# Squares of v summed by transfers, the mixing of gMLP spread over three u chunks, and gelu times mixed v on VectorE

## What is computed

```
z = gelu(rms_norm(x) @ w_in + b_in);  u, v = z[:, :2048], z[:, 2048:]
v = rms_norm(v) * v_gain                     # over the 2048 columns; also an output, for the samples
s[chunk, i, group, d] = sum_j tril(w_s[group])[i, j] * v[chunk, j, group, d] + b_s[group, i]
x = x + (u * s) @ w_out                      # chunks of 128 tokens, 8 groups of 256 columns
```

## Time and profile before

| | us |
|---|---|
| median of 3 runs | 2080.99 |
| the runs | 2080.99, 2080.2, 2087.7 |
| profiled execution, its time | 2089.98 |
| its span, first to last instruction | 2088.1 |
| busy: TensorE, VectorE | 2042.7, 1677.0 |
| busy: ScalarE, GpSimd | 1170.7, 372.2 |

### The profile page before, as it was taken

The page is one execution under the profiler, slowest core; times in us unless marked ns, Lnnn a source line. Parts: engine busy times, 40 slices in busy tenths (PEclk is TensorE's granted clock), DMA queues, the critical chain, the costliest instruction groups (busy, mean ns, idle before and its releaser), DMA issues.

```text
span 2088.1 us, 44481 instructions
## 1 busy us (share of the span) xinstructions
PE 2042.7 (98%) x16512; PEld 1972.9 (94%) x16512; DVE 1677.0 (80%) x2836; ACT 1170.7 (56%) x2101; POOL 372.2 (18%) x413
## 2 busy tenths in 40 slices
PE   9999999989999999999999999999999999999998
PEld 8999999988999999999999999998768889999998
DVE  6779887887477998998899998679665468989997
ACT  5446565666264655655665655445564346656555
POOL 0011111333131111110111111111122121111111
PEclk9999999999999999999999999999999999999999
DMA  5467775664445777775777777451322126777775
GB/s 160 123 162 179 181 184 149 148 152 122 112 112 128 175 179 176 181 186 151 168 177 181 178 186 181 129 138 28 96 72 81 61 61 158 179 184 176 187 181 128
DMA packets 385039, 307.52 MB, mean 147 GB/s; under 512 B 22951, under 2 KB 346836, under 8 KB 384628
## 3 DMA queue, kind: packets, MB, share of 16 engines
q1 hardware_dynamic: 343418, 231.03, 37.0%
q0 software_dynamic: 41152, 74.09, 21.9%
q10 hardware_dynamic: 314, 0.37, 0.1%
HBM read 228.76 MB, written 2.66 MB: 111 GB/s over the span
## 4 chain that ended last, share of the span: by engine, by line
PE 79%; DVE 6%; DMA 6%; issue 4%; ACT 2%; POOL 1%; SPq 1%; DVEq 0%; ACTq 0%; POOLq 0%
PE side L842 29%; PE main L842 20%; PE main L792 16%; DMA raw<-raw 2%; PE side L1389 2%; DVE w_lo L2197 2%; PE main L1151 2%; DMA sums_w<-raw 1%; DMA raw<-in_ffn_w_down 1%; PE main L1319 1%; PE side L1359 1%; POOL tmp_act L3222 1%; DMA raw<-in_ffn_w_gate 1%; PE side L1241 1%; PE main L1221 1%
## 5 line engine op out<-in xcount | busy, mean ns | idle before, releaser
L842 PE MATMUL side<-xw_hi,w_hi 128*128 128x260 f32 x1600 | 455.0, 284 | 20.1 <-DVE v L2347 9.2
L842 PE MATMUL side<-xw_hi,w_lo 128*128 128x260 f32 x1600 | 453.5, 283 | 0.0
L842 PE MATMUL side<-xw_lo,w_hi 128*128 128x260 f32 x1600 | 452.4, 283 | 0.0
L2197 DVE TENSOR_TENSOR w_lo<-raw,w_hi 128x512 fp32r<-128x512 f32 (+2 forms) x540 | 382.8, 709 | 71.0 <-ACT w_hi L1518 22.2
L842 PE MATMUL main<-xw_hi,w_hi 128*128 128x260 f32 x1200 | 341.5, 285 | 0.0
L842 PE MATMUL main<-xw_lo,w_hi 128*128 128x260 f32 x1200 | 338.9, 282 | 0.0
L842 PE MATMUL main<-xw_hi,w_lo 128*128 128x260 f32 x1200 | 338.7, 282 | 0.0
L842 PEld LDWEIGHTS side<-xw_hi,w_hi 128*128 128x128 f32 x1600 | 301.4, 188 | 25.6 <-DVE w_lo L2197 8.5
L842 PEld LDWEIGHTS side<-xw_hi,w_lo 128*128 128x128 f32 x1600 | 301.3, 188 | 0.0
L842 PEld LDWEIGHTS side<-xw_lo,w_hi 128*128 128x128 f32 x1600 | 301.0, 188 | 0.0
L2197 DVE TENSOR_TENSOR w_lo<-sums_w,w_hi 128x1024 fp32r<-128x1024 f32 (+2 forms) x264 | 250.3, 948 | 3.2 <-ACT w_hi L1501 3.2
(11 more groups left out here) (485 smaller groups left out, 4895.2 us busy)
## 6 DMA issues: line engine op xcount, KB each, us to landing
sums_w<-raw POOLq DMA_DIRECT2D x128, 256.0 KB, 3.3
raw<-raw POOLq DMA_DIRECT2D x128, 256.0 KB, 4.9
raw<-in_ffn_w_gate SPq DMA_DIRECT2D x86, 256.0 KB, 4.6
raw<-in_ffn_w_gate SPq DMA_DIRECT2D x43, 512.0 KB, 5.9
raw<-in_ffn_w_up SPq DMA_DIRECT2D x84, 256.0 KB, 4.7
raw<-in_ffn_w_up SPq DMA_DIRECT2D x42, 512.0 KB, 6.0
raw<-in_ffn_w_down SPq DMA_DIRECT2D x56, 256.0 KB, 4.4
raw<-in_ffn_w_down SPq DMA_DIRECT2D x28, 512.0 KB, 5.9
```

Of the source, the lines that this page charges most:

```text
L842: mm = nc.tensor.matmul(into[j], w_tiles(w, weights_at(s, j))[:, k, :], moving[:, k, order[j], :], start=(j in (0, 1) and k == 0 and i == ...
L2197: a = nc.vector.tensor_tensor(dst, src, hi.bitcast(F32), ALU.subtract)
```

## The change

- Squares: chunk 0's go straight into two sums, `square_sum` and `tmp_mul[:, 0]`; those of chunks 1 to 6 are added by two accumulating transfers from GpSimd, one on each chain; those of chunk 7 by VectorE, which also joins the chains (`v_sums`, three adds in the mixing hook of g0). ScalarE squares behind its third snapshot instead of the second. GpSimd adds nothing itself.
- Order: turn of group g at the end of chunk g, copies, mix, bias and product in chunk g + 1, first part and rest in g + 2. The first output products stand behind g4 instead of g3 (`U_FIRST`), the second behind g7, where groups 6 and 7 are finished together. Output products take their last four parts as they come (`late=4`).
- gelu(u) is made in place, in `gm_in` and `tmp_act` by turns; VectorE multiplies it by the mixed v.
- The samples' mixed rows are made once for all groups (`sample_mixes`, `sm_all`); the samples' v rows are scaled by ScalarE.
- In the u chunks the rest of the pair is taken behind L2347 (`rest_late=True`).

Cut to its core (indentation reduced):

```diff
-for q in range(2):
-    for c in range(n_u // 2):
-        free = (l + 5 * c - 6, l + 5 * c - 5) if c >= 2 or q == 0 else (l - 1 + c, l - 1 + c)
-        load_fast(c % 2, w_in, (c + q * n_u // 2) * WC, *free)
-        if q == 0 and c == 1:
-            sp.wait_ge(sum_done, at_gmlp.sums + GT)
-            sp.dma_start(bs_all, gmlp_b_s[0].partition_broadcast(P)).then_inc(bias_in, 16)
-    n, l = n + n_u // 2, l + 5 * (n_u // 2)
-    for i, free in enumerate((l - 5, l, l + 2, l + 3)):
-        load(n + i, i % 2, gmlp_w_out[0], q * KC, KC, i * WC, free)
-    n, l = n + 4, l + 5
+for g in range(NG):
+    free = (l - 6, l - 5) if g not in (U_FIRST, U_FIRST + 1) else (l - 1, l - 1) if g == U_FIRST else (l - 5, l - 5)
+    load_fast(n % 2, w_in, g * WC, *free)
+    if g == 1:
+        sp.wait_ge(sum_done, at_gmlp.sums + GT)
+        sp.dma_start(bs_all, gmlp_b_s[0].partition_broadcast(P)).then_inc(bias_in, 16)
+    n, l = n + 1, l + 5
+    if g in (U_FIRST - 1, NG - 1):
+        q = g // U_FIRST
+        for i, free in enumerate((l - 5, l, l + 2, l + 3)):
+            load(n + i, (n + i) % 2, gmlp_w_out[0], q * KC, KC, i * WC, free)
+        n, l = n + 4, l + 5
...
+def first_turn():
+    rms_v()
+    turn_v(0)()
 for g in range(NG):
-    if g == 0:
-        between = {5: rms_v, 6: turn_v(0, e - 4)}
-    elif g == 1:
-        between = {1: mix(0), 3: turn_v(1, e - 4), 6: mix(1)}
-    else:
-        between = {2: turn_v(g, e if g == NG // 2 else e - 4), 5: mix(g)}
-    fast_chunk(g % 2, e, l, sn, None, between)
+    between = {5: mix(g - 1), 7: turn_v(g)} if g else {7: first_turn}
+    if g == U_FIRST - 1:
+        between.pop(7)
+    elif g == U_FIRST:
+        between[2] = turn_v(g - 1, e)
+    elif g == NG - 1:
+        between.update({6: turn_v(g), 7: mix(g)})
+    fast_chunk((n_v + g + 4 * (g >= U_FIRST)) % 2, e, l, sn, None, between)
     e, l, sn = e + 4, l + 5, sn + 3
-    if g % (NG // 2) == NG // 2 - 1:
-        q = g // (NG // 2)
+    if g in (U_FIRST - 1, NG - 1):
+        q = g // U_FIRST
         for i in range(4):
-            down(l + 1 + i, e + 2 * i, at_gmlp.h + q * KC, KC, slot=i % 2, hi=hv[:, q * KC:(q + 1) * KC, :])
+            down(l + 1 + i, e + 2 * i, at_gmlp.h + q * KC, KC, slot=i % 2, hi=hv[:, q * KC:(q + 1) * KC, :], late=4)
...
     def go():
-        if c:
-            act.wait_ge(sum_done, at_gmlp.sums + 2 * c)
         act.wait_ge(act_done, at_gmlp.act + 2 * c + 2)
+        if c == 0:
+            nc.scalar.activation(square_sum[:], v[:, 0, :], ACT.Square).then_inc(square_done, 1)
+            nc.scalar.activation(tmp_mul[:, 0, :], v[:, 1, :], ACT.Square).then_inc(square_done, 1)
+            return
+        if c >= 2:
+            act.wait_ge(v_added[0], 16 * (c - 1))
+            act.wait_ge(v_added[1], 16 * (c - 1))
         nc.scalar.activation(square[:], v[:, 2 * c:2 * c + 2, :], ACT.Square).then_inc(square_done, 2)
...
-    steps = {2: v_squares(c - 1)}
+    steps = {"scales": v_squares(c - 1)}
...
+        if g >= 2:
+            act.wait_ge(vs_out[g % 2], 16 * (g // 2))
+        nc.scalar.activation(vs_tok[:, g % 2, :, :].rearrange("p m c -> p (m c)"), side[0:NS, 2, 0:2 * P], ACT.Copy,
+                             scale=rv[0:NS, QB + NS:QB + NS + 1]).then_inc(v_seen, 1)
...
-    last = g % (NG // 2) == NG // 2 - 1
+    last = g in (U_FIRST - 1, NG - 1)
     if g == 0:
-        steps = {2: v_squares(n_v - 1), 4: v_root}
+        steps = {"scales": v_squares(n_v - 1)}
+        after = [lambda: nc.scalar.activation(primed[:, 0:1], eps[:, 0:1], ACT.Sqrt), v_root]
     elif g == 1:
-        steps = {3: v_copies(1, (0, 1)), 4: h_copies(0)}
+        steps = {"scales": v_copies(0), 4: u_gelu(0, e - 4)}
+        after = [u_gelu(1, e)]
     else:
-        steps = {"turn": v_copies(g, (0,)), "scales": v_copies(g, (1,))}
-        if g != NG // 2:
-            steps[2] = h_copies(g - 1)
-    fast_chunk(g % 2, 16 * ((n + 1) // 2 + 1), t, e, w, "plain" if last else "fast", steps=steps)
-    if g == 0:
-        v_copies(0, (0, 1))()
-    u_gelu(g)
+        steps = {"scales": v_copies(g - 1)}
+        if g != U_FIRST:
+            steps[1] = h_copies(g - 2)
+        after = [u_gelu(g, e)]
+    if g == U_FIRST - 1:
+        after = [h_copies(g - 1), u_gelu(g, e)]
+    elif g == NG - 1:
+        after = [v_copies(g), u_gelu(g, e), h_copies(g - 1), h_copies(g)]
+    fast_chunk(n % 2, 16 * ((n + 1) // 2 + 1), t, e, w, "plain" if last else "fast", steps=steps)
+    for step in after:
+        step()
     n, t, e, w = n + 1, t + 7, e + 4, w + 2
-    if last:
-        h_copies(g)()
-    if g == NG // 2 - 1:
...
-def sample_gains():
+def v_sums():
     dve.wait_ge(square_done, at_gmlp.sums + GT)
     vs = v[:, :, SEQ:TOK]
     nc.vector.tensor_tensor(vs, vs, bc(v_gain, NS), ALU.mult).then_inc(vg_done, 1)
+    nc.vector.tensor_tensor(square[:, 0, :], square[:, 0, :], square[:, 1, :], ALU.add).then_inc(sum_done, 1)
+    for m in range(2):
+        dve.wait_ge(v_added[m], 16 * (n_v - 2))
+    nc.vector.tensor_tensor(square_sum[:], square_sum[:], tmp_mul[:, 0, :], ALU.add).then_inc(sum_done, 1)
+    dve.wait_ge(sum_done, at_gmlp.sums + 2)
+    nc.vector.tensor_tensor(square_sum[:], square_sum[:], square[:, 0, :], ALU.add).then_inc(sum_done, GT - 2)
+def v_scales():
     dve.wait_ge(root_done, at_gmlp.rms + 2)
     nc.vector.reciprocal(rv[:, 0:QB + NS], rv_root[:, 0:QB + NS])
     nc.vector.reciprocal(rv[0:NS, QB + NS:QB + NS + 1],
                          rv_root[0:NS, QB + NS:QB + NS + 1]).then_inc(rstd_done, 1)
+def sample_mixes():
+    by_group = sm_all[:, :, :].rearrange("p (g m) b -> p g (m b)", m=2)
+    dve.wait_ge(rstd_done, at_gmlp.rms + 2)
+    dve.wait_ge(vg_done, 1)
+    dve.wait_ge(bias_in, 48)
+    nc.vector.tensor_tensor(sm_all[:], v[:, :, SEQ:TOK], rv[:, QB:QB + NS].unsqueeze(1).to_broadcast([P, GT, NS]),
+                            ALU.mult).then_inc(vg_done, 1)
+    dve.wait_ge(vg_done, 2)
+    nc.vector.tensor_tensor(by_group, by_group, bc(ws_first[:, :], 2 * NS), ALU.mult).then_inc(vg_done, 1)
+    dve.wait_ge(vg_done, 3)
+    nc.vector.tensor_tensor(by_group, by_group, bc(bs_first[:, :], 2 * NS), ALU.add).then_inc(vg_done, 1)
+    dve.wait_ge(vg_done, 4)
 def mix(g):
     def go():
-        dve.wait_ge(v_turned, g + 1)
         if g == 0:
-            dve.wait_ge(rstd_done, at_gmlp.rms + 2)
-            dve.wait_ge(vg_done, 1)
-            dve.wait_ge(bias_in, 48)
-        if g >= 2:
-            dve.wait_ge(vs_out[g % 2], 16 * (g // 2))
-        nc.vector.tensor_scalar(vs_tok[:, g % 2, :, :], side[0:NS, 2, 0:2 * P].rearrange("p (m c) -> p m c", m=2),
-                                rv[0:NS, QB + NS:QB + NS + 1], None, ALU.mult).then_inc(v_seen, 1)
...
+        for m in range(2):
+            j = 2 * g + m
+            h = gelu_u[g % 2][:, m, :]
+            dve.wait_ge(act_done, a + GT + j + 1)
+            dve.wait_ge(mixed, j + 1)
+            nc.vector.tensor_tensor(h, h, tmp_mul[:, m, :], ALU.mult).then_inc(mul_done, 1)
...
-    last = g % (NG // 2) == NG // 2 - 1
-    def ready(g=g):
-        if g:
-            dve.wait_ge(act_done, a + GT + 2 * g)
-        if g >= 2 and g != NG // 2:
-            rests(g - 1)()
-    hooks = dict(mixing=mix(g)) if g >= 2 else dict(own=mix(0), held=mix(1), behind=rests(0)) if g else \
-        dict(mixing=sample_gains)
-    fast_chunk(g % 2, 16 * ((n + 1) // 2 + 1), t, e, l, w, sn, natural(gm_in), rstd_rows, "plain" if last else "fast",
-               ready=ready, **hooks)
+    hooks = dict(mixing=mix(g - 1)) if g else dict(mixing=v_sums)
+    if g == 1:
+        hooks["start"] = v_scales
+    if g >= 2:
+        def free(g=g):
+            if g != U_FIRST:
+                rests(g - 2)()
+            dve.wait_ge(h_lo_done, at_gmlp.h + 2 * g - 2)
+        hooks["ready"] = free
+    fast_chunk(n % 2, 16 * ((n + 1) // 2 + 1), t, e, l, w, sn, natural(gelu_u[g % 2]), rstd_rows,
+               "plain" if g in (U_FIRST - 1, NG - 1) else "fast", rest_late=True, **hooks)
     n, t, e, l, w, sn = n + 1, t + 7, e + 4, l + 5, w + 2, sn + 3
-    if last:
-        rests(g)()
-    if g == NG // 2 - 1:
+    if g == U_FIRST - 1:
+        rests(g - 1)()
...
+mix(NG - 1)()
+rests(NG - 2)()
+rests(NG - 1)()
...
 def add_v_squares(c):
-    for m in range(2):
-        add_squares(m, at_gmlp.sums + 2 * c + m, c == 0 and m == 0)
+    pool.wait_ge(square_done, at_gmlp.sums + 2 * c + 2)
+    if c >= 2:
+        for m in range(2):
+            pool.wait_ge(v_added[m], 16 * (c - 1))
+    pool.dma_start(square_sum[:], square[:, 0, :], accum_op=ALU.add).then_inc(v_added[0], 16)
+    pool.dma_start(tmp_mul[:, 0, :], square[:, 1, :], accum_op=ALU.add).then_inc(v_added[1], 16)
...
 def multiply(g):
     pool.wait_ge(v_seen, g + 1)
     pool.dma_start(new_v[0, :, 0, 2 * g * P:2 * (g + 1) * P], vs_tok[:, g % 2, :, :].rearrange("p m c -> p (m c)"))\
         .then_inc(vs_out[g % 2], 16)
-    for m in range(2):
-        j = 2 * g + m
-        pool.wait_ge(act_done, at_gmlp.act + GT + j + 1)
```

(12 more changed lines are left out.)

80 lines of the change are left out of this document (45 added, 35 removed).

## The result

The changed kernel takes 2091.09 us (median of 17 runs, 2086.63 to 2094.02), the kernel before 2085.53 us (17 runs on the same chips, 2080.20 to 2089.59). The ratio is 1.0026 with a 95% interval from 1.0018 to 1.0034: 5.4 us slower, where 6.0 us faster were forecast. By the bound of 0.5% that is no difference, as was thought likeliest; but it lies outside the range, on the other side. 4.5 us of the distance to the 2075.0 belong to the kernel before, whose median over 17 runs is that much above the 2080.99 of the three runs that the forecast started from; with them taken off, 2086.6 is still above 2083. The best version of the experiments takes 20 us less than the kernel before.

What follows compares the result with a forecast made beforehand. The prediction took a v chunk to be bound by VectorE held up by GpSimd. 8.9 (v chunks) - 1.5 (DMA) - 1.4 (u chunks) = 6.0 us off 2080.99 gave 2075.0 us; range with rivals 2067 to 2083.

Steps and rivals of the forecast that it cites:

- The v chunks' own gain, 8.9 us: Third to eighth v chunk: without GpSimd's adds the seventh product no longer waits, 8.9 us free if weights are there.
- rival C: v chunks: L2214 stays long because GpSimd's issues hold VectorE; v gains nothing, 2082.4 us; chance 0.08.
- The DMA engines, 1.5 us: v chunks: added transfers of squares fill the DMA engines; 4.8 - 3.3 = 1.5 us lost.
- 3.3 us of slack: v chunks: weight sums may land about 1.8 and 1.5 us later before TensorE waits; used once.
- the upper bound of 4.8: v chunks: 0.8 us lost in each of six chunks if packets of the two queues don't overlap.
- g0's tail: End of g0: VectorE makes the sum of squares, ending at 11.6 us; TensorE loses 1.5 us.
- g1's seventh product: g1: g2's weights, queued on SP behind the later sum and the bias, delay the seventh product by 2.7 us.
- the turn behind it: g1: the turn after the seventh product waits for VectorE's mix until 17.2 us, another 2.7 us lost.
- g7's turn: g7: the turn of group 7 waits for the mix of group 6 until 14.3 us; 4.1 us lost.
- the output product: End of g4: VectorE's product delays the last evacuation ahead of the output product; 4.4 us lost, where 3.2 were.
- B: v chunks: DMA engines cannot carry the weights and squares, a chunk takes 13.5 us; 2093.9 us; chance 0.08.
- A: g1: g2's weights are in time, 13.5 instead of 18.3 us, and no 1.5 us DMA loss; 2068.7 us; chance 0.30.

Runs made afterwards that it cites:

- e2_no_transfers: The changed kernel without the accumulating transfers of squares, so the sum lacks v chunks 1 to 6; 1.0002 of the kernel before.
- e1_order: The changed kernel with SP loading g2's weights ahead of the wait for the sum of squares and the bias; 0.9990 of the kernel before.
- e10_sums: The changed kernel with the edits of e4_all_vector, e1_order and e12_changed_last, and g0's sum of squares shortened; 2065.37 us, 0.9904 of the kernel before.
- e11_fill: The changed kernel with the edits of e4_all_vector and e1_order, plus unread matmuls in waits of g0, g7 and ahead of the first output product; 0.9924.
- e3_fill: The changed kernel with 67 unread matmuls in TensorE's waits in g1, ahead of the first output product and in g7; 0.9991 of the kernel before.
- e7_before_order: The kernel before with g2's weights loaded ahead of the wait for the sum of squares and the bias; 1.0002 of the kernel before.
- e4_all_vector: The changed kernel with VectorE adding all squares of v, and no transfers for squares; 0.9998 of the kernel before.
- e5_pair: The changed kernel with VectorE adding a v chunk's two squares together, then one accumulating transfer instead of two; 1.0016 of the kernel before.
- e12_changed_last: The changed kernel with another order of ScalarE's and VectorE's work in g4 and g7 alone; 0.9976 of the kernel before.

## Why the prediction was wrong, point by point

**The v chunks' own gain, 8.9 us: right.** Without traffic they take 61.51 us, and 61.5 was the forecast's lower end. The hand-made schedule holds: in a chunk of e2_no_transfers that starts at 415.0 the third evacuation ends at 423.4 (8.4 us on, forecast 8.3) and the seventh product starts 8.6 us on. The Trainium skill, "GPSIMD Engine Reference", section "Key points", says that GpSimd contends with VectorE instructions that have two SBUF inputs; the trace agrees, 1585 ns beside GpSimd's adds and 685 without, and rival C is out.

**The DMA engines, 1.5 us: the step that failed first.** The step was the subtraction: 4.8 us of DMA time less 3.3 us of slack, since the two weight sums could land 1.8 and 1.5 us later unnoticed. They land in 6.8 and 6.6 us (medians of the v chunks of the changed kernel), where it was 3.3 us for both in those of the kernel before: 3.5 and 3.3 us later, twice the slack. (The forecast slack itself was not right either: in e2_no_transfers the outer sum lands in 5.5 us, 2.2 later than in the kernel before, the inner one in 3.3 as there, and TensorE waits for neither.) The squares' transfers themselves take 6.6 and 7.3 us, not the 4 to 6 of the prediction's signs. The slack carried the first chunks (no wait from 400 to 420 us), then TensorE waited for L1591, and once more in g0, so that g0 takes 15.82 us and not 14.0. A v chunk takes 11.06 us, above the 11 that the prediction had named as the sign that it is wrong. That the 4.85 us of e2_no_transfers are so near the upper bound of 4.8 is luck: 1.6 of them are the lower clock, and other profiles have 3.1 and 4.4. Nor do the runs show that the 16 engines are what is short, as the prediction had it: SP's loads of 256 KB into `raw` land in 4.6 us with the squares' transfers and in 5.0 without them, so only GpSimd's accumulating transfers got slower by them. Whether its queue or the engines are the limit was not separated. By the figures of the Trainium skill, "DMA: Bandwidth & Descriptors", section "Anatomy of one DMA", the transfers would have cost nothing, as an estimate; the runs show otherwise.

**The waits in the u chunks: right in place, most of them in size.** g0's tail 1.63 (forecast 1.5), g1's seventh product 3.03 (2.7), the turn behind it 1.13 (2.7), g7's turn 3.67 (4.1), the output product 1.02 + 2.40 (4.4 with the chunk's other losses). g1 has a third wait, 1.17 us for ScalarE's L1609, that was not forecast. g2 takes 14.4 us (forecast 13.5; 1.4 of it clock), g3 13.0 (13.5), g5 14.0 (13.9), g6 13.0 (13.1). The chain of g1 over SP's wait, the bias and the weights is shown by e1_order.

**What was missing: the price behind a wait.** Every wait was counted once, as idle time. All the rows of before, with waits up to 1.92 us, have a clock of 1.00, and I took that for a property of waits. The changed kernel has fewer of them in the v chunks and four longer ones, and about 8 us of its profiled execution are lost to matmuls at the lower clock. This is the second failed step: the term was put at nothing without a reason. In g1, work and waits come to 18.28 us, forecast 18.3, measured 21.22; that the first two agree is luck, since the unforecast 1.17 and a turn that waits 1.6 less, in part because the slow seventh product fills its wait, cancel.

**The sum.** Forecast -6.0. Added: v chunks 3.4 (1.6 of it clock), g0 1.8, g1 2.9 (2.3 clock), g2 to g4 0.0 (43.21 against 43.2: 1.4 us of clock, as much won on the chunks), output products 1.5 (clock; 47.49 against 46.47 less the 0.5 of waits), g5 to g7 1.5 (1.4 of it clock). That makes +5.1; the medians say +5.4. Of the 11.1 us the traffic has 3.6 (v chunks without clock, and g0) and the clock about 8; the rest nearly cancels, 0.6 more in g1 against 1.4 less in g2 to g4, where the forecast had rounded upwards. These are figures of one execution, of the lowest mean clock; over all runs the clock's part is nearer 6 us.

**The rivals.** B (the DMA engines cannot carry the v chunks) had the right place at a quarter of its price: a chunk takes 11.06 us instead of 10.25 without the traffic, and not 13.5. A (g2's weights in time) did not happen. None of the rivals ended slower for the reason that decided here.

## What to carry to other kernels

- Price a wait of TensorE with what comes behind it. Several short waits may be cheaper than one long one of the same sum, so a change that gathers waits can lose although it takes more idle time away than it adds (here 18.7 us of idle became 17.9, and the stage took 5.2 us more). Filling a long wait with matmuls that nobody reads is a quick test for this, and bought 0.4% here.
- Read slack from landing times, not from the busy time of the DMA engines: with two more accumulating transfers a chunk the weight sums landed 3.3 to 3.5 us later than before, while the busy time said 0.8 us a chunk. And ask first whether an engine with gaps can do the work in place: VectorE took these adds for nothing.
- In a queue in order, look at what stands behind a wait before moving what it waits for: one line on SP was worth 7.5 us here, and nothing in the kernel before.

## What the runs showed of the hardware that was not expected

**The length of a wait does not decide whether the lower clock follows.** The same wait stands in many of the profiles, each of one execution. Behind the turn's wait of 3.65 to 3.67 us in g7, all seven profiles that have it show matmuls at the lower clock. Behind the 2.4 us ahead of the first output product it is three of six (47.5 us for the products instead of 46.0). Behind the 1.63 us in g0 it is eight of ten. Behind 0.8 us (e10_sums) and behind the filled waits (e11_fill, and in e3_fill those of g4 and g7) it is none. The kernel before is not free of it: with its waits of 1.9 us ahead of output products, the profile of e7_before_order shows 47.48 us for the first and a clock of 0.85 behind the second. But the wait of 1.60 us (1.61 in the kernel before) for the third evacuation of the second v chunk, as long as that of g0, stands in all 14 profiles, and no matmul at the lower clock follows in any. Behind 2.4 to 2.5 us at the turn of g1 it is two of five (e3_fill and e4_all_vector, not e2_no_transfers, e5_pair and e12_changed_last). What decides from place to place, and from one execution to another, was not found.

**The clock explains only a part of the spread of the times.** The kernel before ran in 2079.85 to 2090.97 us (35 runs), e10_sums in 2064.25 to 2067.37 (5 runs, too few to compare). Over the 35 runs a mean clock higher by 0.001 goes with a time shorter by 1.5 us, with a correlation of -0.51: about a quarter of the scatter. Over the 17 runs of the changed kernel it is -0.20.

**Accumulating transfers slow one another.** With the squares' transfers in the queue a weight sum of 256 KB needed 7.0 us from issue to the release of the next (434.22 to 441.21); without them 3.6 us (e2_no_transfers), for the same bytes. The loads that SP issues beside them did not get slower (4.6 us with the squares' transfers, 5.0 without).
